# Three weight units by block at each stage boundary, and new work lists for ScalarE, VectorE and GpSimd around the first and last feed-forward tile

## The chip, the cores and the metric

The kernel runs on one core of one Trainium2 chip. TensorE multiplies, ScalarE (ACT in the profile), VectorE (DVE) and GpSimd (POOL) compute elementwise, SyncE (SP) issues the DMAs. Each engine works through its own list of instructions in the order of the program and waits on semaphores. The metric is the device time of one execution in microseconds; for the kernel before, three runs gave a median of 3314.09 us (3314.05 to 3314.48).

## The reference

One step of a two-layer encoder on 1024 new frames and 32 frames of a running stream (1056 columns together), model width 1024. What matters here is the frame around the two attentions, which is the same in both layers:

```python
y = o @ w_oa[i]                       # layer 0; w_ob in layer 1
r = r + rms_norm(y, g_mix_post[i])
# SwiGLU feed-forward, 2816 wide, between two norms, added to r
# gated input embedding: p @ w_ple, gated by sigmoid(norm(r) @ w_ple_gate),
# normed (g_ple_post) and added to r
```

Each norm divides a column of 1024 values by its root mean square. Layer 1 then takes keys, values and forget values from r (w_kb, w_vb, w_f) and attends once more.

## The kernel before

Everything is transposed: 128 rows of the width on the partitions, eight such tiles (`KD`), and the 1056 columns in three blocks b of 352 (`NB`, `TB`). Each float32 operand is split in two parts, high and low, and a product is three matmuls (`three`), so that one *group*, 1024 rows deep, is 24 matmuls of 352 columns. A weight unit is 128x1024: it is loaded to `wraw`, copied to `wh` (high) and subtracted to `wl` (low), mostly by GpSimd (L791, L796), in three slots.

A norm of a block passes all engines. ScalarE squares the eight tiles (L1429), the squares are added up on VectorE (L1885) or GpSimd (L818, the list `POOL_SUMS` says which) through a ring of two buffers, so that a square waits for the sum two before. `cols` (L979) has TensorE add over the partitions, `root` (L1437) takes the root on ScalarE, `inverse` (L1895, L1899) the reciprocal and a diagonal on VectorE, `spread` (L993) carries it to all partitions on TensorE. A "post" norm then scales the sublayer's output (`scaled`, L1909, VectorE), `residual` (L827, GpSimd) adds it to r. A "pre" norm of the new r needs no scaling ahead of the matmul: `high` (L1462, ScalarE) and `low` (L1924, VectorE) split r times the gain at once, the product is formed, and the reciprocal root, kept by `keep` (L1443) in `rsp`, multiplies the product afterwards (`gate`, `mul`: L2140, L2145).

The order of work is written out by hand for each engine. The stages of a layer after attention are:

- output projection, 24 groups. `PLACES` gives their order: six units over all three blocks, then units 6 and 7 block by block (`by_place`), so that block 0 finishes first and its norm can start.
- feed-forward, 22 tiles (`ffn_pe`, `ffn_act`, `ffn`). A tile is a gate group and an up group per block, with 24 `down` products (three matmuls each) of the tile before between them. `first_tile` goes block by block as the blocks' `low` parts come; the first group of `second_tile` writes the bank of the first gate product and waits for `silu(0,0)` (L1633), which has read it. `last_tile` goes block by block too and puts its own block 0 `down` products in (`E_AT2`).
- embedding, 24 short groups (`ple`, six matmuls each), interleaved with the first gate unit's groups; then the gate projection, 24 groups in the order of `PLACES`, with `scale` (L2260), `sigmoid` (L1765), `gated` (L2266).
- in layer 0, the key, forget and value projections (`kb`, `wf`, `vb`) then follow; layer 1 ends with the last norm, the last `residual` and six stores of the output.

Names such as "pre 0" below mean the pre norm of block 0.

## Time and profile before

| | |
|---|---|
| median of three runs | 3314.09 us |
| profiled execution | 3314.65 us, its span 3312.9 us |
| TensorE busy | 3077.6 us (93%) |
| VectorE, GpSimd, ScalarE busy | 2008.1, 1479.0, 979.6 us |
| mean granted TensorE clock | 0.962 of full |

The span goes from the first to the last instruction. Below, a stretch is named by its place in it in microseconds: layer 0's attention ends near 690, its feed-forward runs to about 1550, its gate projection to 1700, keys and values follow, and layer 1 repeats this from 2290 on. A wait in brackets, as in `[19.39 <-ACT ffn_act L1633]`, is idle time of that engine just before the row's instruction and what ended it.

### The profile page before, as it was taken

How to read it: one execution, taken by the hardware profiler on the slowest of the kernel's cores; microseconds unless marked ns; L12 is line 12 of the kernel's file. 1: busy time of each engine (PE TensorE's matmuls, PEld its weight loads, DVE VectorE, ACT ScalarE, POOL GpSimd, SP SyncE). 2: the span in 40 equal slices, each digit the busy share in tenths (PEclk: the TensorE clock that was granted, in tenths of full speed). 3: DMA queues.
4: the chain of work that ended last, by engine and by line, in shares of the span. 5: the costliest groups of instructions: out<-in, count | busy, mean ns of one | idle time of the engine just before them, and what ended most of it. 6: DMA issues, size and time to landing. Idle time of an engine off the chain costs nothing.

```text
span 3312.9 us, 59033 instructions
## 1 busy us (share of the span) xinstructions
PE 3077.6 (93%) x21250; PEld 2979.3 (90%) x21250; DVE 2008.1 (61%) x3637; ACT 979.6 (30%) x2248; POOL 1479.0 (45%) x963
## 2 busy tenths in 40 slices
PE   7898999997999999997888999999799999999787
PEld 6888999987999999997887888888799999999777
DVE  5555777456565565555573677754655655656555
ACT  3233666433000000003442167753300000000242
POOL 5223454464333343335565455545443333433454
PEclk9999999998999999998998999999899999999889
DMA  3387444211111111111102565622011111111101
GB/s 107 138 302 239 124 120 134 77 64 33 44 44 51 44 45 43 44 51 46 39 26 98 181 146 129 142 79 71 26 52 38 44 51 44 47 42 38 65 32 53
DMA packets 163119, 264.69 MB, mean 80 GB/s; under 512 B 95040, under 2 KB 108880, under 8 KB 162624
## 3 DMA queue, kind: packets, MB, share of 16 engines
q1 hardware_dynamic: 163008, 263.21, 25.8%
q8 instruction: 70, 1.15, 0.2%
q14 instruction: 41, 0.34, 0.0%
HBM read 197.74 MB, written 65.42 MB: 79 GB/s over the span
## 4 chain that ended last, share of the span: by engine, by line
PE 79%; DVE 7%; POOL 4%; issue 4%; ACT 3%; DMA 2%; SPq 1%; ACTq 0%; DVEq 0%; POOLq 0%
PE ps L1225 29%; PE ps L958 14%; PE ps L959 14%; PE ps L960 14%; PE ps L1135 4%; POOL pre_sums L818 2%; DVE sublayer_out L1909 1%; DVE pre_sums L1885 1%; PE ps L1105 1%; PE ps L993 1%; POOL residual L827 1%; DVE act_lo L1924 1%; PE ps L1106 1%; PE ps L979 1%; DMA kA_lo<-stage_lo 1%
## 5 line engine op out<-in xcount | busy, mean ns | idle before, releaser
L791 POOL TENSOR_TENSOR weight_hi<-weight_raw,ones 128x1024 fp32r<-128x1024 f32 x194 | 384.5, 1982 | 1243.8 <-PE ps L960 648.3
L2136 DVE TENSOR_TENSOR sublayer_out<-ps,sublayer_out 128x352 f32<-128x352 f32 x1008 | 527.8, 524 | 536.1 <-PE ps L960 527.8
L1225 PE MATMUL ps<-act_hi,weight_hi 128*128 128x352 f32 x2112 | 690.2, 327 | 54.6 <-ACT ffn_act L1633 38.5
L1225 PE MATMUL ps<-act_lo,weight_hi 128*128 128x352 f32 x2112 | 684.9, 324 | 0.0
L1225 PE MATMUL ps<-act_hi,weight_lo 128*128 128x352 f32 x2112 | 684.6, 324 | 0.0
L958 PE MATMUL ps<-act_hi,weight_hi 128*128 128x352 f32 (+2 forms) x1392 | 472.0, 339 | 46.2 <-POOL weight_lo L796 19.8
L796 POOL TENSOR_TENSOR weight_lo<-weight_raw,weight_hi 128x1024 fp32r<-128x1024 f32 x201 | 498.2, 2478 | 24.5 <-ACT weight_hi L1623 9.3
L858 POOL TENSOR_TENSOR probs<-probs,row_inv 128x1024 f32<-128x1024 f32 (+8 forms) x288 | 310.6, 1092 | 351.5 <-DVE row_inv L2083 351.4
L959 PE MATMUL ps<-act_lo,weight_hi 128*128 128x352 f32 (+2 forms) x1392 | 456.9, 328 | 0.0
L960 PE MATMUL ps<-act_hi,weight_lo 128*128 128x352 f32 (+2 forms) x1392 | 456.5, 328 | 0.0
L1225 PEld LDWEIGHTS ps<-act_hi,weight_hi 128*128 128x128 f32 x2112 | 400.3, 190 | 58.6 <-issue 50.5
L1225 PEld LDWEIGHTS ps<-act_lo,weight_hi 128*128 128x128 f32 x2112 | 401.2, 190 | 1.4 <-issue 1.0
L1225 PEld LDWEIGHTS ps<-act_hi,weight_lo 128*128 128x128 f32 x2112 | 400.7, 190 | 0.4 <-issue 0.2
L958 PEld LDWEIGHTS ps<-act_hi,weight_hi 128*128 128x128 f32 (+2 forms) x1392 | 265.5, 191 | 59.3 <-issue 37.4
L2088 DVE TENSOR_TENSOR probs_t_lo<-ps,probs_t_hi 128x512 fp32r<-128x512 f32 (+3 forms) x448 | 220.2, 498 | 95.6 <-ACT probs_t_hi L1587 92.7
L958 PE MATMUL ps<-probs_t_hi,v_hi 128*64 128x128 f32 (+2 forms) x1248 | 272.6, 246 | 1.4 <-DVE act_lo L2095 0.9
L959 PEld LDWEIGHTS ps<-act_lo,weight_hi 128*128 128x128 f32 (+2 forms) x1392 | 266.3, 191 | 5.9 <-issue 1.8
L960 PEld LDWEIGHTS ps<-act_hi,weight_lo 128*128 128x128 f32 (+2 forms) x1392 | 265.5, 191 | 2.9
L1633 ACT ACTIVATE ffn_act<-ps 128x352 f32<-128x352 f32 x132 | 61.4, 465 | 653.9 <-DVE ps L2140 653.9
L960 PE MATMUL ps<-probs_t_hi,v_lo 128*64 128x128 f32 (+2 forms) x1248 | 242.2, 221 | 0.0
L959 PE MATMUL ps<-probs_t_lo,v_hi 128*64 128x128 f32 (+2 forms) x1248 | 241.9, 221 | 0.0
L1578 ACT ACTIVATE probs<-ps,neg_max 128x1024 f32<-128x1024 f32 (+8 forms) x288 | 204.4, 710 | 99.5 <-DVE neg_max L2075 89.9
(168 smaller groups left out, 6201.2 us busy)
## 6 DMA issues: line engine op xcount, KB each, us to landing
weight_raw<-units SPq DMA_DIRECT2D x201, 512.0 KB, 3.3
k_hi<-kB_hi SPq DMA_DIRECT2D x32, 328.0 KB
qA_hi<-stage_hi SPq DMA_DIRECT2D x16, 528.0 KB, 2.7
qA_lo<-stage_lo SPq DMA_DIRECT2D x16, 528.0 KB, 4.0
q_hi<-qA_hi SPq DMA_DIRECT2D x16, 528.0 KB
q_lo<-qA_lo SPq DMA_DIRECT2D x16, 528.0 KB
kA_hi<-stage_hi SPq DMA_DIRECT2D x8, 656.0 KB, 3.0
kA_lo<-stage_lo SPq DMA_DIRECT2D x8, 656.0 KB, 4.6
```

Source lines behind the costliest of these rows:

```text
L791: pool.tensor_tensor(wh[:, slot, :], wraw[:, slot, :], ones[:, 0:1].to_broadcast((P, UW)), ALU.mult).then_inc(w_hi[slot], 1)
L796: pool.tensor_tensor(wl[:, slot, :], wraw[:, slot, :], wh[:, slot, :].bitcast(F32), ALU.subtract).then_inc(w_rdy[slot], 1)
L818: pool.tensor_tensor(sum_tile(key), sum_tile(key), square_tile(key, j), ALU.add).then_inc(n_add[1], 1)
L858: pool.tensor_tensor(p, p, rinv[0:M, k:k + 1].to_broadcast((M, KEYS[tile])), ALU.mult).then_inc(at_p, 1)
L958: nc.tensor.matmul(out, ah, bh, start=first, stop=False)
L959: nc.tensor.matmul(out, ah, bl, start=False, stop=False)
L960: return nc.tensor.matmul(out, al, bh, start=False, stop=last)
L1135: mm = nc.tensor.transpose(ps[0:kr, 4 + c % 2, j * P:j * P + M], pr[0:M, PROB_AT[tile] + kt * P:PROB_AT[tile] + kt * P + kr], ident[0:M, 0:M])
L1225: mm = nc.tensor.matmul(ps[:, 3 * slot + b, 0:TB], a, x, start=(k == 0 and pas == 0), stop=(k == KD - 1 and pas == 2))
L1578: nc.scalar.activation(pr[0:M, PROB_AT[tile]:PROB_AT[tile] + KEYS[tile]], score_tile(tile), ACT.Exp, bias=nmx[0:M, k:k + 1], accum_out=rsu ...
L2088: last = V.tensor_tensor(dst, src, hi.bitcast(F32), ALU.subtract)
L2136: V.tensor_tensor(y[:, m, c], src, y[:, m, c], ALU.add).then_inc(f_acc, 1)
```

## The change

The change keeps every matmul of the feed-forward and of the projections, and every load. It alters orders and who does some of the elementwise work:

- `PLACES`: five units over all blocks, then units 5, 6 and 7 by block. `cols` and `spread` of the post norms stand at other products.
- Pre norms of the stages s2, s3, s5, s6: ScalarE squares blocks 0 and 1 in turn, with block 1 in the other ring; GpSimd adds blocks 0 and 2 of s2 and s5 and block 0 of s3 and s6, VectorE the rest. In s4 block 1 goes to VectorE.
- First tile: `cols` and `spread` of pre 0 leave it and stand, with those of pre 1, ahead of the second tile. `silu(0,0)` comes before the last squares of block 2.
- Last tile: gate 0, gate 1, up 0, up 1, gate 2, up 2. `down` of block 2 alternates with `scaled` of block 0 on VectorE and with three `ple` groups on TensorE. VectorE makes the low parts of the two `pe` units, ScalarE the high part of the first `pg` unit, GpSimd its low part before the sums of post 2.
- ScalarE gets one more activation, a square root of one column, in the last tile. It also makes the high parts of more units (`split_high`), GpSimd keeps their low parts.
- In layer 0's end `vb` 0 is multiplied by its gain later, after the sums of pre 2.

```diff
-PLACES = [(m, b) for m in range(6) for b in range(NB)] + [(m, b) for b in range(NB) for m in (6, 7)]
+LATE = (5, 6, 7)
+PLACES = [(m, b) for m in range(LATE[0]) for b in range(NB)] + [(m, b) for b in range(NB) for m in LATE]
...
+    if _s in ALTERNATE:
+        SQUARES += [((_s, "pre", b), j) for j in range(KD) for b in range(2)] + [((_s, "pre", 2), j) for j in range(KD)]
...
+def ring_of(key):
+    s, kind, b = key
+    return "pre" if kind == "pre" and not (b == 1 and s in ALTERNATE) else "post"
...
+LAST_ORDER = [(0, 0), (0, 1), (1, 0), (1, 1), (0, 2), (1, 2)]
```

GpSimd ahead of the feed-forward (`tail_pool`):

```diff
-                split(0, u[0], (lin_rd, unit_done(lin, 5)))
                 residual((f"s{s}", "post", 0))
+                low(0, u[0])
+                residual((f"s{s}", "post", 1), 0, 4)
                 low(1, u[1])
-                residual((f"s{s}", "post", 1))
+                residual((f"s{s}", "post", 1), 4)
                 residual((f"s{s}", "post", 2))
                 adds((f"s{s}", "pre", 0))
-                adds((f"s{s}", "pre", 1))
+                low(0, u[0] + 1)
+                adds((f"s{s}", "pre", 2))
```

TensorE, ahead of the second tile:

```diff
+                    cols((s, "pre", 0))
+                    spread((s, "pre", 0))
+                    cols((s, "pre", 1))
+                    spread((s, "pre", 1))
```

TensorE, after the last tile's gate and up groups:

```diff
-                    for d in range(KD, 2 * KD):
+                    for d in range(KD, 3 * KD):
                         down(f, par, d, True)
-                        if d == KD + 3:
+                        if d == KD + 4:
                             cols((key, "post", 0))
...
+                        if d in (2 * KD + 2, 2 * KD + 4, 2 * KD + 6):
+                            ple(0, (d - 2 * KD - 2) // 2)
+                    spread((key, "post", 1))
```

TensorE, second gate unit:

```diff
-                place(gate, 1, 0, among=[(2, do(spread, pre[1])), (6, do(cols, pre[2]))])
-                place(gate, 1, 1, among=[(2, do(spread, pre[2]))])
-                place(gate, 1, 2)
+                place(gate, 1, 0, among=[(4, do(cols, pre[0]))])
+                place(gate, 1, 1, among=[(0, do(spread, pre[0])), (4, do(cols, pre[1]))])
+                place(gate, 1, 2, among=[(0, do(spread, pre[1])), (6, do(cols, pre[2]))])
+                spread(pre[2])
```

ScalarE, last tile:

```diff
+                for m in range(4):
+                    y_square(0, m)
+                silu(f, 2)
+                split_high(0, u[0], (fg_rd, 3 * (f0 + NF)))
+                nc.scalar.activation(epsc[:, 1:2], epsc[:, 0:1], ACT.Sqrt)
```

VectorE, after the last tile:

```diff
+                inverse(post[0])
+                for j in range(KD):
+                    down(NF - 1, 2 * KD + j, last=True)
+                    scaled(post[0], j, j + 1)
```

VectorE, last entries ahead of the feed-forward:

```diff
                 inverse(pre[0])
-                adds(pre[2])
+                for j in range(6, KD):
+                    add(pre[1], j)
+                inverse(pre[1])
```

ScalarE at the start of layer 0's feed-forward, before: from the last `act_hi` copies of r to the first silu (`ffn_act`). `pre_sums` and `pre_squares` are squares of a pre norm, `root` and `pre_rstd` are `root` and `keep`.

```order
L1462 ACTIVATE act_hi<-residual,gains 128x352 x12
L1429 ACTIVATE pre_sums_90<-residual 128x352
L1429 ACTIVATE pre_squares<-residual 128x352 x7
L1429 ACTIVATE pre_sums_90<-residual 128x352
L1429 ACTIVATE pre_squares<-residual 128x352 x3
L1437 ACTIVATE root<-ps,eps_col 88x4
L1429 ACTIVATE pre_squares<-residual 128x352 x4
L1443 ACTIVATE pre_rstd<-ps 128x352
L1429 ACTIVATE pre_sums_90<-residual 128x352
L1429 ACTIVATE pre_squares<-residual 128x352 x7
L1633 ACT_TABLE_LOAD
L1633 ACTIVATE ffn_act<-ps 128x352
```

The same place after the change, from the last weight copy on (`post_squares` is here the ring of block 1):

```order
L1452 ACTIVATE pre_sums_90<-residual 128x352
L1452 ACTIVATE pre_squares<-residual 128x352 x2
L1460 ACTIVATE root<-ps,eps_col 88x4
L1466 ACTIVATE pre_rstd<-ps 128x352
L1452 ACTIVATE pre_squares<-residual 128x352 x2
L1460 ACTIVATE root<-ps,eps_col 88x4
L1452 ACTIVATE pre_squares<-residual 128x352
L1466 ACTIVATE pre_rstd<-ps 128x352
L1656 ACT_TABLE_LOAD
L1656 ACTIVATE ffn_act<-ps 128x352
L1452 ACTIVATE pre_squares<-residual 128x352 x2
L1656 ACTIVATE ffn_act<-ps 128x352
```

Before, all squares of block 2 stand ahead of the first silu. After, six of them do, in two pieces between the roots of blocks 0 and 1, and two follow it; the pairs of blocks 0 and 1 stand above.

GpSimd between the last feed-forward tile and the gate projection of layer 0, before:

```order
L818 TENSOR_TENSOR post_sums<-post_sums,post_squares 128x352 x7
L796 TENSOR_TENSOR weight_lo<-weight_raw,weight_hi 128x1024
L818 TENSOR_TENSOR post_sums<-post_sums,post_squares 128x352 x7
L827 TENSOR_TENSOR residual<-residual,sublayer_out 128x352 x8
L796 TENSOR_TENSOR weight_lo<-weight_raw,weight_hi 128x1024
L818 TENSOR_TENSOR post_sums<-post_sums,post_squares 128x352 x7
L827 TENSOR_TENSOR residual<-residual,sublayer_out 128x352 x8
L791 TENSOR_TENSOR weight_hi<-weight_raw,ones 128x1024
L796 TENSOR_TENSOR weight_lo<-weight_raw,weight_hi 128x1024
L827 TENSOR_TENSOR residual<-residual,sublayer_out 128x352 x8
L818 TENSOR_TENSOR pre_sums_91<-pre_sums_91,pre_squares 128x352 x7
```

and after:

```order
L834 TENSOR_TENSOR post_sums<-post_sums,post_squares 128x352 x14
L843 TENSOR_TENSOR residual<-residual,sublayer_out 128x352 x8
L812 TENSOR_TENSOR weight_lo<-weight_raw,weight_hi 128x1024
L834 TENSOR_TENSOR post_sums<-post_sums,post_squares 128x352 x7
L843 TENSOR_TENSOR residual<-residual,sublayer_out 128x352 x16
L834 TENSOR_TENSOR pre_sums_91<-pre_sums_91,pre_squares 128x352 x7
L807 TENSOR_TENSOR weight_hi<-weight_raw,ones 128x1024
```

Two `weight_lo` (the `pe` units) and one `weight_hi` leave GpSimd. The low part of the first gate unit moves from behind `residual` of block 1 to behind that of block 0, and the sums of post 2 now all stand ahead of `residual` of block 1.

## Rows read from the trace of the kernel before

**Rows 1.** the page: the span

```profile
span 3312.9 us, 59033 instructions
```

**Rows 2.** TensorE's waits over the span: total, times, longest

```profile
PE ps L1225 <- ACT ffn_act L1633: 38.5, 2, 19.4
PE ps L993 <- DVE rstd_diagonal L1899: 33.5, 14, 5.8
```

**Rows 3.** stretches: length, busy per engine (instructions), clock, DMA share, GB/s

```profile
1527.00:1631.00 104.00, 76.29 (x390) 70.81 (x390) 63.14 (x101) 50.99 (x113) 70.40 (x59) 0.79 0.16 57
1684.00:1773.00 89.00, 69.42 (x385) 57.16 (x383) 60.87 (x90) 40.36 (x81) 68.17 (x56) 0.87 0.03 9
```

**Rows 4.** the same view, the steady feed-forward

```profile
790.00:1470.00 680.00, 679.79 (x4240) 679.50 (x4239) 404.29 (x713) 59.51 (x122) 256.57 (x116) 1.00 0.13 44
```

**Rows 5.** TensorE's timeline: start, us, instruction [idle before it <-releaser]

```profile
778.35 0.63 PE L1225 MATMUL ps<-act_hi,weight_hi 128*128 128x352 f32 x1 [19.39 <-ACT ffn_act L1633]
```

**Rows 6.** ScalarE's timeline, opening of layer 0's feed-forward

```profile
745.46 0.59 ACT L1462 ACTIVATE act_hi<-residual,gains 128x352 fp32r<-128x352 f32 x1 [0.59 <-POOL residual L827]
...
749.31 0.50 ACT L1429 ACTIVATE pre_squares<-residual 128x352 f32<-128x352 f32 x1 [0.69 <-POOL pre_sums L818]
...
770.00 0.50 ACT L1429 ACTIVATE pre_squares<-residual 128x352 f32<-128x352 f32 x1 [1.64 <-DVE pre_sums L1885]
...
785.09 1.28 ACT L1633 ACT_TABLE_LOAD   x1
786.38 0.46 ACT L1633 ACTIVATE ffn_act<-ps 128x352 f32<-128x352 f32 x1
```

**Rows 7.** VectorE's timeline there

```profile
736.36 2.06 DVE L1909 SCALAR_TENSOR_TENSOR sublayer_out<-sublayer_out,gains,ps 128x352 f32<-128x352 f32 x4 [1.16 <-PE ps L993]
...
763.30 6.67 DVE L1885 TENSOR_TENSOR pre_sums<-pre_sums,pre_squares 128x352 f32<-128x352 f32 x3 [0.18 <-ACT pre_squares L1429]
...
781.51 0.17 DVE L1895 RECIPROCAL rstd<-root 88x4 f32<-88x4 f32 x1 [2.69 <-ACT root L1437]
781.72 0.52 DVE L1899 TENSOR_TENSOR rstd_diagonal<-ident,rstd 88x352 f32<-88x352 f32 x1
```

**Rows 8.** GpSimd's timeline there

```profile
737.92 7.50 POOL L827 TENSOR_TENSOR residual<-residual,sublayer_out 128x352 f32<-128x352 f32 x7
746.90 7.04 POOL L818 TENSOR_TENSOR pre_sums<-pre_sums,pre_squares 128x352 f32<-128x352 f32 x6 [1.48 <-ACT pre_squares L1429]
...
764.95 2.50 POOL L796 TENSOR_TENSOR weight_lo<-weight_raw,weight_hi 128x1024 fp32r<-128x1024 f32 x1
```

**Rows 9.** TensorE's timeline, end of layer 0's feed-forward (last row: layer 1)

```profile
1530.74 0.43 PE L958 MATMUL ps<-ffn_hi_odd,weight_hi 128*128 128x352 f32 x1 [3.67 <-DVE sublayer_out L2136]
...
1577.47 0.63 PE L958 MATMUL ps<-act_hi,weight_hi 128*128 128x352 f32 x1 [7.76 <-issue]
...
1612.70 1.54 PE L993 MATMUL ps<-rstd_diagonal,ones 88*128 88x352 f32 x2 [5.45 <-DVE rstd_diagonal L1899]
...
3164.13 0.63 PE L958 MATMUL ps<-act_hi,weight_hi 128*128 128x352 f32 x1 [7.77 <-issue]
```

**Rows 10.** GpSimd's timeline there

```profile
1572.61 2.17 POOL L791 TENSOR_TENSOR weight_hi<-weight_raw,ones 128x1024 fp32r<-128x1024 f32 x1
...
1593.43 7.45 POOL L818 TENSOR_TENSOR pre_sums<-pre_sums,pre_squares 128x352 f32<-128x352 f32 x7 [7.71 <-ACT pre_squares L1429]
```

**Rows 11.** VectorE's timeline there

```profile
1603.52 8.49 DVE L1885 TENSOR_TENSOR pre_sums<-pre_sums,pre_squares 128x352 f32<-128x352 f32 x5
...
1635.30 0.53 DVE L2260 TENSOR_TENSOR ps<-ps,pre_rstd 128x352 f32<-128x352 f32 x1 [1.43 <-PE ps L960]
```

**Rows 12.** TensorE's timeline, keys of layer 0

```profile
1747.44 1.54 PE L993 MATMUL ps<-rstd_diagonal,ones 88*128 88x352 f32 x2 [5.76 <-DVE rstd_diagonal L1899]
```

**Rows 13.** GpSimd's timeline there

```profile
1770.29 2.57 POOL L796 TENSOR_TENSOR weight_lo<-weight_raw,weight_hi 128x1024 fp32r<-128x1024 f32 x1
```

**Rows 14.** TensorE's timeline, last norm of layer 1

```profile
3297.31 1.33 PE L979 MATMUL ps<-ones,post_sums 128*88 128x1 f32 x8 [5.27 <-DVE post_sums L1885]
```

## What the change is predicted to do

> **What bounds the kernel now.** I read the page first: the span is 3312.9 us [rows 1], TensorE is busy for 93% of it, and the chain that ended last is 79% TensorE. So the matmuls are the bound except where TensorE sits idle. The stretches come next. In the steady feed-forward 4240 matmuls take 679.79 of 680 us, 0.160 us each, at full clock [rows 4]: nothing is to be had there, and the change leaves it alone. Between the stages it is otherwise: TensorE is busy for 76.29 of 104 us at the end of layer 0's feed-forward (granted clock 0.79 on average) and for 69.42 of 89 us at the keys (0.87) [rows 3]. The list of waits names the largest: 38.5 us in two waits for a silu, up to 19.4 us, and 33.5 us in 14 waits for the diagonal of a norm [rows 2]. Both are in the norms between the stages, where ScalarE, VectorE and GpSimd pass small work to each other. The timelines then say why.
>
> **Opening of the feed-forward (twice).** TensorE stands for 19.39 us before the second tile at 778.35 [rows 5]; the reader sees that it waits for `silu(0,0)`, which frees the bank. ScalarE's list has all squares of block 2 ahead of it, and VectorE's sums between them go in steps of about 2.3 us (three from 763.30 in 6.67 us), in step with GpSimd's weight operations (one 2.50 us from 764.95) [rows 7, 8], so ScalarE's square at 770.00 waits 1.64 us [rows 6].
> After the change I walk the same chain. Post 2 is scaled at 736.36 before [rows 7]. Three units by block give the earlier blocks one more group (24 x 0.160 = 3.8 us) of cover, but `cols` of post 2 moves from product 12 to 28 and VectorE has sums and `low` before it; I get 734, so 2.4 earlier. The last copy of r ends at 745.46 + 0.59 - 2.4 = 743.6 [rows 6]. Then seven pairs of sums for blocks 0 and 1: GpSimd alone takes 7.04 / 6 = 1.17 us per sum [rows 8]; with VectorE's sum beside it I take 1.3 (bounds 1.17 and, if each pair went by a weight operation, 2.50). 7 x 1.3 = 9.1, two squares first 0.8, and two weight copies moved to ScalarE about 1 beyond what the ring hides: 754.5. From there `cols` (1.33 at most [rows 14], I take 0.8 at full clock), the root 0.3 (four columns, less than the silu's 0.46), reciprocal and diagonal 0.17 + 0.52 [rows 7], `spread` 0.8 (half of the two in 1.54 [rows 9]): 757.1. VectorE has two sums of block 1 left behind `inverse` of pre 0, beside one weight operation of GpSimd (up to 2.50): 759.3. `cols` of pre 1: 760.1. Its root is queued behind two squares of block 2, which wait for GpSimd's first sums after that weight operation: this is the wait that the change adds, and `keep` of pre 1 and the silu are behind it; 760.7. Diagonal, `spread`, `keep`: 762.7. Table load 1.28, silu 0.46 [rows 6]: 764.4. So the second tile starts **14 us** earlier, though the first tile, without `cols` and `spread` of pre 0 and the wait for post 2, ends only about 6 earlier than 778.35 - 19.39 = 759.0, and TensorE still waits about 11 us. Bounds: 7 x (2.50 - 1.3) = 8.4 less, so 5.6; and 16 if the sums go at 1.17 and the copies are hidden. Weights for it are ready: `low` of slot 0 comes right after the sums of pre 0. What is late next is `cols` of pre 2 at product 6, perhaps 0.5 us, and it is within the 14. Layer 1 repeats it: its wait is the other half of the 38.5 [rows 2]. Term: 28, bounds 11 and 32.
>
> On ScalarE's table loads: the row at 785.09 takes 1.28 us and the next activation starts at 786.38 [rows 6], so a switch costs 1.28 here. The Trainium skill, "ScalarE: Activation LUTs", section "What ACT_TABLE_LOAD costs", gives about 1283 ns and a drain of about 1380 ns more for each switch. By that page the silu would come 1.4 us later in each layer and the sum would be about 3 us less. The trace shows the load and no drain, so the sum goes by 1.28.
>
> **End of the feed-forward and embedding (twice).** Before, TensorE waits 3.67 us at 1530.74 (block 2's high part stands behind block 0's squares), 7.76 at 1577.47 for the first gate unit's weights, whose GpSimd work starts only at 1572.61, and 5.45 at 1612.70 for the diagonal of pre 0 [rows 9, 10]. The sums of pre 1 on VectorE, five of them over 8.49 us from 1603.52, come after those of pre 0, seven in 7.45 us from 1593.43 [rows 10, 11]. The third gate unit's first group starts one group before its `scale` at 1635.30, so at 1631.4 [rows 11]; I compare that point.
> After: the last tile's products end at about the same 1527. High part 2 still waits for block 0's squares, but these start earlier: about 1.5 of the 3.67 stay. VectorE gets two 1024-column subtractions that the trace doesn't show on VectorE; the bounds are 0.52 (a 352-column one [rows 7]) and 2.50 (GpSimd's own [rows 8]), I take 1.2 each, nearer to the first since it is the same engine. `down` of block 2 alternates with `scaled`, 8 x 1.0 us, and ends at 1546, some 3 us earlier with three `ple` groups done. The first gate unit's weights are ready at about 1550, so the 7.76 goes; what is late next is the sums of post 2, at 1559 to 1564, since the last five squares are queued behind eight `take`s of `ple` results. GpSimd then does `residual` of block 1 at about 1.07 each (7.50 / 7 [rows 8]): 1568 to 1572, then of block 2: 1576 to 1581. The copies and `take`s follow, and ScalarE squares pairs 3 to 7 only after the last `take` of block 2 (1582 at full clock). Sums of pre 0 done at 1588, and only then GpSimd's two operations for gate unit 1, ready at 1593: TensorE waits about 5 there. The rest (`cols`, `spread`, the sums of pre 1 and pre 2 beside three weight splits) gives 1610 to 1612 for the third unit's start at full clock. At half clock all through, 144 `ple` and 144 gate matmuls would cost 0.16 more each, 46 us, of which I find half hidden in the waits above: 1634. Some waits end on a slow matmul (0.63 for the first after the 7.76), others on a fast one (0.43) [rows 9], and the mean clock was 0.79 [rows 3]; I take a third of the way: 1618, **13 us** earlier. Bounds: -3 and 21. Layer 1 is the same stage with the same waits (7.77 at 3164.13 [rows 9]). Term: 26, bounds -5 and 42.
>
> **Keys in layer 0.** TensorE waits 5.76 us for the diagonal of pre 0 at 1747.44 [rows 12]. After, `cols` of post 1 moves to an earlier place of its unit and waits longer by about 2 (one more `scaled` half and a table load lie before its sum), the second key unit's weights come late (about 3), and `residual` of block 2 stands behind five sums. Pre 1 goes to VectorE, so the last `spread` comes about 9 earlier. But `vb` 0's gain now stands behind the sums of pre 2: gain, split, gain, split (six operations of 128x1024 at 2.17 to 2.57 each, 13 in all [rows 8, 10, 13]) end at about 1768, where they ended at 1772.9 [rows 13]. Both are needed for the value groups. Term: 5, bounds -4 (the weights' 2.57 twice and a waiting sum more) and 9.
>
> **Last norm.** The third unit's cover lets the sum before `cols` at 3297.31, with a wait of 5.27 [rows 14], come about 1 us earlier; after it nothing changes. Term: 1, bounds 0 and 2.
>
> **Sum.** 28 + 26 + 5 + 1 = 60. The profiled execution took 3314.65 us, 0.56 above the median of 3314.09; 3314.65 - 60 = 3254.65, and as a median 3254. All terms at a bound would be 2 and 85, which don't fall together.
>
> **Rivals.**
> *The end of the feed-forward gives nothing.* For it: GpSimd is left with one list, in which sums of post 2, three residuals, sums of pre 0 and the gate unit's weights now stand in one line, and a `take` there waits for a residual that waits for the sums. Against: the 7.76 and 5.45 waits have their causes removed. It gives 3254 + 24 = 3278.
> *The clock stays full and the sums overlap freely.* Twice 16 and twice 19, keys 8, last norm 1: 79 less, 3235. Against it: TensorE still waits some 11 us at each opening.
> *The port.* Slower than before: VectorE's and GpSimd's sums, now side by side, hold each other up. For it: VectorE's 2.3 us steps above. Against: these were beside 2.50 us operations; GpSimd's residuals slowed only to 1.07. There are five places with seven pairs. If a pair cost 1.3 + x in place of 1.3, 35x reaches 60 at x = 1.7, so it decides from 3.0 us a pair on. With a GpSimd weight operation and a sum one after the other, 2.50 + 7.45 / 7 = 3.56 [rows 8, 10], it gives 35 x 2.26 = 79 against 60: 3333.
> The Trainium skill, "SBUF — State Buffer", section "Who interferes with whom", states the mechanism: a VectorE instruction with two SBUF inputs and a GpSimd instruction that reads SBUF exclude each other for the whole instruction. By that rule the trace agrees as to the steps, and a pair would cost the two durations one after the other, 1.06 + 0.52 = 1.6, not 3.56; with 1.6 the sum would be 10 less.
> *The change doesn't do what it says*, since another wait of the same size (weights for the second tile, or block 2's sums) takes the silu's place: only the other terms are left, 32, so 3282.
>
> **Chances.** Forecast (a gain of 45 to 75) 0.58; the end gives nothing 0.14; free overlap 0.15; another wait at the opening 0.08; the port 0.02; smaller gains or none of several causes 0.03. What a measurement can tell from no change is 0.2%, 6.6 us. Slower by more than that 0.03, within it 0.03, faster 0.94. The range takes in the first two rivals: 3230 to 3284.
>
> **What would show it.** TensorE's wait before the second tile should be about 11 us, not 19.4, in both layers, and end on a silu about 14 us earlier after the attention's end. VectorE's sums of pre 1 at the opening should come at about 1.3 us each beside GpSimd's. The 7.76 wait should be gone, and a wait of some us for GpSimd's weights should be at gate unit 1. `cols` of post 1 in layer 0's gate projection should wait longer than before. If the pairs take over 2 us, or the wait before the second tile stays above 17, the walk of the first term is wrong; if the third gate unit starts less than 5 us earlier after the last tile, the second is.

## The result and the profile after

The changed kernel takes 3262.60 us (median of 4 runs, 3261.40 to 3267.74) against 3314.28 us (4 runs, 3314.05 to 3315.22) of the kernel before in the same series: 51.7 us less, a ratio of 0.9844 with a 95% interval of 0.9832 to 0.9856. The forecast was 3254 with a range of 3230 to 3284. The time is in the range, 8.6 us above the forecast, but the sum came out near it partly by luck. The stages that the forecast counted on gave 34.6 us in place of its 60: the opening was put too high, and keys and last norm went the other way. What brought the total near was a gain of 16 us in a stage to which the forecast had given nothing.

The page of the kernel after begins with its span; 46.9 us less than in [rows 1].

```profile
span 3266.0 us, 59087 instructions
```

TensorE's waits over the span, in total, how many, longest. They answer to [rows 2].

```profile
PE ps L975 <- POOL weight_lo L812: 24.8, 8, 15.0
PE ps L996 <- DVE post_sums L1951: 23.7, 7, 6.0
PE ps L1010 <- DVE rstd_diagonal L1965: 22.6, 11, 7.0
PE ps L975 <- issue: 14.7, 3, 7.1
...
PE ps L1261 <- ACT ffn_act L1656: 4.8, 2, 2.4
```

The 38.5 us for a silu are down to 4.8, and the 33.5 us for a norm's diagonal to 22.6. The stretches of [rows 3], from the last products of the last tile to the third gate unit (now 90 us long, 104 before), and the 89 us ahead of the value products:

```profile
1514.00:1604.00 90.00, 70.24 (x390) 65.10 (x390) 62.82 (x96) 47.03 (x104) 67.86 (x57) 0.89 0.18 66
1665.00:1754.00 89.00, 64.68 (x354) 54.17 (x352) 63.20 (x90) 36.33 (x77) 62.10 (x47) 0.85 0.08 29
```

The first holds the same 390 matmuls in 14 us less, at a granted clock of 0.89 and not 0.79. In the second TensorE is busy for less of the time than before: the keys have become worse.

Where the time went is best read from milestones, each the same instruction in both traces. Four of the anchors in after, and one in before, from TensorE's timeline: the start of attention (302.03 and 305.76), the second tile, the third gate unit and the value products.

```profile
302.03 0.80 PE L958 MATMUL ps<-k_hi,q_hi 128*128 128x512 f32 x1 [9.68 <-DVE q_turned L2046]
```

```profile
305.76 0.80 PE L975 MATMUL ps<-k_hi,q_hi 128*128 128x512 f32 x1 [9.67 <-DVE q_turned L2112]
...
773.15 0.63 PE L1261 MATMUL ps<-act_hi,weight_hi 128*128 128x352 f32 x1 [2.42 <-ACT ffn_act L1656]
...
1604.24 0.63 PE L975 MATMUL ps<-act_hi,weight_hi 128*128 128x352 f32 x1 [2.96 <-DVE sublayer_out L2356]
...
1754.18 0.55 PE L975 MATMUL ps<-weight_hi,act_hi 128*128 128x256 f32 x1 [0.60 <-issue]
```

The profiled execution of after is 3.7 us late at the attention already, ahead of all that the change touches (it is also the slowest of its four). So stages are compared by their length, and whole traces from this start to the end of the span: 3010.9 us before, 2960.2 after, 50.7 less.

| stage (layer 0 / layer 1) | before, us | after, us | difference | predicted |
|---|---|---|---|---|
| opening: output projection to second tile | 153.8 / 153.5 | 144.7 / 144.9 | -17.7 | -28 |
| second tile to the last tile's own first `down` (1515.56 before, 1502.40 after) | 737.2 / 737.8 | 729.3 / 729.5 | -16.3 | 0 |
| from there to the `scale` of the third gate unit's first group (1635.30, 1609.79) | 119.7 / 119.9 | 107.4 / 107.7 | -24.5 | -26 |
| from there to the value products (layer 0) | 139.0 | 144.4 | +5.4 | -5 |
| from there to the last norm's scaling (layer 1) | 79.0 | 81.2 | +2.2 | -1 |

The sum is -50.9; layer 1's attention took 0.2 more.

### The profile page after: what moved, and what is told of

It reads as the page before. It is cut to its first block, busy times and chain, and to the rows that moved or that the text cites. A ratio compares the mean times of both kernels' runs of the same rounds, so it can differ in the third digit from the quotient of the medians.

```text
span 3266.0 us, 59087 instructions
## 1 busy us (share of the span) xinstructions
PE 3078.8 (94%) x21250; PEld 2982.2 (91%) x21250; DVE 1998.0 (61%) x3648; ACT 979.1 (30%) x2255; POOL 1450.5 (44%) x943
## 4 chain that ended last, share of the span: by engine, by line
PE 82%; DVE 7%; issue 3%; ACT 2%; POOL 2%; DMA 2%; SPq 1%; ACTq 0%; DVEq 0%; POOLq 0%
PE ps L1261 30%; PE ps L975 15%; PE ps L976 14%; PE ps L977 14%; PE ps L1152 4%; DVE sublayer_out L1975 1%; PE ps L1122 1%; PE ps L996 1%; PE ps L1010 1%; PE ps L1123 1%; DVE act_lo L1990 1%; POOL pre_sums L834 1%; DMA kA_lo<-stage_lo 1%; DVE pre_sums L1951 1%; DVE stage_lo L2071 1%
## 5 line engine op out<-in xcount | busy, mean ns | idle before, releaser
L807 POOL TENSOR_TENSOR weight_hi<-weight_raw,ones 128x1024 fp32r<-128x1024 f32 x185 | 366.5, 1981 | 1187.8 <-PE ps L977 616.3
L812 POOL TENSOR_TENSOR weight_lo<-weight_raw,weight_hi 128x1024 fp32r<-128x1024 f32 x197 | 486.9, 2471 | 38.9 <-ACT weight_hi L1646 24.4
```

Of the source, the lines that this page charges most:

```text
L807: pool.tensor_tensor(wh[:, slot, :], wraw[:, slot, :], ones[:, 0:1].to_broadcast((P, UW)), ALU.mult).then_inc(w_hi[slot], 1)
L812: pool.tensor_tensor(wl[:, slot, :], wraw[:, slot, :], wh[:, slot, :].bitcast(F32), ALU.subtract).then_inc(w_rdy[slot], 1)
```

## The experiments

All were timed beside the kernel before. "From the attention's start" is the span minus the start of the row that [..q_turned] releases, as above; two executions of the same kernel differ by up to 7 us in it, so single traces are read by stage, where they agree better.

**e1: only the place of a wait, in the kernel before.** The trace of before has a gap that no term of the prediction spoke of. TensorE's timeline there, and GpSimd's:

```profile
1483.24 0.63 PE L1225 MATMUL ps<-act_hi,weight_hi 128*128 128x352 f32 x1 [5.24 <-issue]
```

```profile
1480.64 2.50 POOL L796 TENSOR_TENSOR weight_lo<-weight_raw,weight_hi 128x1024 fp32r<-128x1024 f32 x1
```

```
-                    for slot in range(2):
-                        pe.wait_ge(w_rdy[slot], f + (u[slot] + 1))
                     for b in range(NB):
                         for slot in range(2):
+                            pe.wait_ge(w_rdy[slot], f + (u[slot] + 1))
                             products(f, slot, b, 24 * (2 * b + slot), among)
```

> The kernel before, with one thing changed: in the last feed-forward tile TensorE waits for the up projection's weights (slot 1) right ahead of its first up group, and no longer ahead of all groups. Theory A (TensorE's 5.24 us of 'issue' at 1483.24 are that wait: GpSimd's weight_lo of slot 1 ends at 1480.64 + 2.50 = 1483.14): one gate group of 24 matmuls, 3.86 us, runs in it, so 1.4 us of the wait stay, and most of the 1.9 us of half clock behind it go; 4 to 6 us in each layer, 8 to 12 in all: 3302 to 3306 us, and in the trace no wait over 2 us there. Theory B (the 5.24 us are a stall of instruction supply or of the clock, not a wait for weights): within 2 us of before, and the gap stays.

Measured: 3303.18 us (3298.36 to 3305.66), ratio 0.9964 [0.9950, 0.9978]. From the second tile to the last tile's `down` wait 730.7 and 730.6 us, where before has 737.2 and 737.8: 13.8 less in both layers. Two stretches of e1 over the place of the gap (columns as in [rows 3]):

```profile
1476.00:1480.00 4.00, 4.00 (x27) 4.00 (x26) 3.40 (x4) 0.50 (x1) 3.92 (x3) 1.00 0.31 73
1480.00:1484.00 4.00, 3.94 (x25) 3.65 (x24) 2.56 (x7) 0.00 (x0) 2.33 (x1) 1.00 0.70 231
```

and of before over it:

```profile
1478.00:1482.00 4.00, 0.00 (x1) 0.00 (x0) 2.35 (x4) 0.50 (x1) 3.92 (x3) 0.80 0.56 197
1482.00:1486.00 4.00, 2.76 (x9) 2.79 (x10) 0.00 (x0) 0.00 (x0) 1.14 (x1) 0.50 0.58 197
```

The gap is gone, and with it the half clock behind it (0.50 in before, 1.00 in e1). Theory A holds. Nothing is left of the wait, not 1.4 us: the first group carries `down` products of the tile before among its own, so it covers more than its 24 x 0.160 us. "Issue" in the list of waits was a wait for weights; it ends 0.10 us after GpSimd's `weight_lo` (1480.64 + 2.50). Of the 13.8 us by stage, 10.8 arrive in the time: in the trace of e1 the next stage is 1.9 and 0.7 us longer than in before (121.6 and 120.6), the keys' 4.2 (143.2), and only part of that is made up by shorter openings (151.1 and 152.0).

**e2: the same wait, put back in the kernel after.**

```
+                    for slot in range(2):
+                        pe.wait_ge(w_rdy[slot], f + (u[slot] + 1))
                     for n, (slot, b) in enumerate(LAST_ORDER):
-                        pe.wait_ge(w_rdy[slot], f + (u[slot] + 1))
                         products(f, slot, b, 24 * n, among)
```

> The kernel after, with the wait for both slots' weights back ahead of all groups of the last feed-forward tile; the new order of the groups stays. Theory A (the order of the waits gives the last tile's 8 us in each layer): about 7 us a layer come back, so 14 over after: 3276 to 3279 us, and the gap of about 5.2 us is there again, named 'issue' or weight_lo. Theory B (the new order of groups, or another edit, gives it): within 3 us of after, 3260 to 3266.

Measured: 3273.87 us (3267.98 to 3275.60), ratio 0.9878 [0.9862, 0.9894]; 11 over after. From the attention's start 2970.8. The stage is 736.3 and 735.4 us long again, and its trace has the gap:

```profile
1471.63 0.63 PE L1261 MATMUL ps<-act_hi,weight_hi 128*128 128x352 f32 x1 [5.24 <-issue]
```

Theory A, from the other side: 12.9 us by stage, and by time 11 and not the 14 that it gave. To the order of the groups by itself and to the other edits is left what separates this stage of e2 from before's, 0.9 and 2.4 us. The order lets two gate groups run ahead of the first up group; e1 shows that one is enough for the wait for the up weights.

**e3: two units by block at the gate projections and before's lists for the keys and the last norm.**

```
 LATE = (5, 6, 7)
+GATE_LATE = (6, 7)
...
+            unit("kb", 0, ("pg0", 5))
...
-            unit_low("kb", 0)
...
+            adds(("s4", "pre", 1))
             adds(("s4", "pre", 2))
```

> The kernel after, with two units by block (6, 7) at the gate projections and the lists of before for layer 0's keys and the last norm; the output projections keep three units. Theory A (by the two traces this part of the change costs 5.4 us at the keys and 2.2 at the last norm): 7 us less than after, about 3255 us. Theory B (these losses come from what is left over of the earlier stages, for instance from the shifted start of the gate projection, and not from this part): within 2 us of after, 3261 to 3265. What was predicted for this part alone was a gain of 6, so 3269 without it.

Measured: 3260.16 us (3254.89 to 3266.33), ratio 0.9843 [0.9829, 0.9857], from the attention's start 2953.8, 6.4 less than after and 1.3 less than its second execution (e12). By time the two can't be told apart (3262.60 in another series); by stage the keys' part is 141.8 us, and 142.3 in e8, which has the same lists. Nine traces with the lists of after (both of after, e2, e4 to e7, e9, e11) lie between 144.1 and 144.5. With before's lists there are four values: 139.0, 143.2 (e1), 141.8 and 142.3. So this part of the change costs 1 to 5 us at the keys, about 2.8 in the mean. The last norm's stage is 79.0, 79.0, 80.5 and 80.3 us with before's lists; with after's it is 81.1 to 81.3 in six traces and 79.6 or 79.7 in three, about 1 us more in the mean. The sign of theory A is borne out at the keys, its size half; at the last norm the two ranges overlap.

**e4: two units by block at the output projections only.**

```
-LATE = (5, 6, 7)
+LATE = (6, 7)
+GATE_LATE = (5, 6, 7)
...
-                take(5, 1)
+                take(6, 1)
...
-                high(pre[0], 0, 2)
...
+                high(pre[0], 0, 3)
```

> The kernel after, with two units by block (6, 7) at the output projections only, with the lists of before up to the scaling of the last post norm; pairs of sums and everything behind stay. Theory A (three units by block moved the scaling of post 2 not at all, 736.67 against 736.36 by the trace, and cost 1.4 us at the start of the first tile): within 2 us of after, or up to 3 less: 3260 to 3264 us. Theory B (as predicted, three units give the scaling 2.4 us of lead in each layer): 4 to 6 us more than after, about 3267.

Measured: 3270.94 us (3266.82 to 3272.01), ratio 0.9868 [0.9852, 0.9884]; from the attention's start 2966.1, 5.9 more than after. The openings take 148.0 and 149.4 us. Theory A falls: after's are 144.7 and 144.9, and the sixteen openings of after's code in eight traces have a mean of 143.9, so three units are worth about 5 us in each layer, at least 3 in any pair of executions. Theory B gave 4 to 6 in all and not by layer, and for a lead of the scaling that isn't there.

The scaling of post 2 comes 113.0 us after the output projection's start in e4, 112.1 in after (110.9 in e12) and 111.8 in before (109.1 in e1). So it has not moved forward, and that is why two traces alone made the third unit look worthless. What it waits for is TensorE's `spread`. In after, and below it in e4, ScalarE's root of post 2 and TensorE's `spread` behind it:

```profile
737.27 0.26 ACT L1460 ACTIVATE root<-ps,eps_col 88x4 f32<-88x4 f32 x1 [5.18 <-PE ps L996]
...
739.75 0.76 PE L1010 MATMUL ps<-rstd_diagonal,ones 88*128 88x352 f32 x2
```

```profile
734.45 0.26 ACT L1468 ACTIVATE root<-ps,eps_col 88x4 f32<-88x4 f32 x1 [8.29 <-PE ps L1004]
...
738.53 0.76 PE L1018 MATMUL ps<-rstd_diagonal,ones 88*128 88x352 f32 x2
```

The root waits for TensorE's `cols`, not for a weight copy on ScalarE, and `spread` starts without a wait: the change has it at product 44 of the first tile (before: 24), and the diagonal lay ready for 1.5 us in after, for 3.1 in e4. In e4 TensorE gets there later since it waits for `act_lo` on the way (1.10, 0.43, 0.44 us), with matmuls 0.29 us apart behind that; and VectorE has twelve `low` left behind the scaling, 10.98 us, where after has ten in 8.65.

**e5: the end of the feed-forward and the embedding as before.** (Diff: the blocks of TensorE's, ScalarE's, VectorE's and GpSimd's programs between the last tile's products and the second gate unit are those of before; its core is)

```
-ALTERNATE = ("s2", "s3", "s5", "s6")
+ALTERNATE = ("s2", "s5")
...
-                unit_low(gate, 0)
+                slot, use, _ = USES[gate, 0]
+                split(slot, use, (fd_rd, 24 * (f0 + NF)))
...
+                    row_squares(pre[1], m, m + 1)
-                pair_squares(3, KD)
```

> The kernel after, with the stage between the last tile and the second gate unit as before: the order of down, cols and spread after the last tile, the places of the embedding groups, ScalarE's, VectorE's and GpSimd's lists there, and the sums of this stage's pre norm not in pairs. The last tile's new order of groups and waits stays. Theory A (this part is worth the 12.3 us in each layer that the two traces show from the last tile to the third gate unit): about 24 us over after, measured from the start of the attention, where the traces of after stands at 2960.2 us before the end: 2984; as a time about 3287. Theory B (part of these 12 us is owed to the last tile's new order, which comes first in the same stretch): 12 to 18 us over after.

Measured: 3285.44 us (3281.62 to 3287.98), ratio 0.9915 [0.9900, 0.9930], 23 over after; from the attention's start 2977.0, 17 over. The two measures disagree, and the stage decides: it takes 119.2 and 119.4 us, against 107.4 and 107.7, so 23.5 us in both layers. Of the 6.7 us between the two, 4.2 are this execution's short openings, in code that is not changed (142.0 and 143.4). Theory A holds; the wait for the first gate unit is back:

```profile
1559.43 0.63 PE L978 MATMUL ps<-act_hi,weight_hi 128*128 128x352 f32 x1 [8.04 <-issue]
```

**e6 and e11: the second gate unit's weights on ScalarE and VectorE.** In after TensorE stands for 7.04 us at 1582.67, called issue; GpSimd's timeline says for what:

```profile
1582.67 0.63 PE L975 MATMUL ps<-act_hi,weight_hi 128*128 128x352 f32 x1 [7.04 <-issue]
```

```profile
1576.21 2.09 POOL L834 TENSOR_TENSOR pre_sums<-pre_sums,pre_squares 128x352 f32<-128x352 f32 x2
1578.26 1.89 POOL L807 TENSOR_TENSOR weight_hi<-weight_raw,ones 128x1024 fp32r<-128x1024 f32 x1
1580.23 2.34 POOL L812 TENSOR_TENSOR weight_lo<-weight_raw,weight_hi 128x1024 fp32r<-128x1024 f32 x1
```

```
-                for j in (1, 2):
-                    slot, use, _ = USES[gate, j]
-                    split(slot, use, (pe_rd, 24 * layer + (20, 24)[j - 1]))
+                slot, use, _ = USES[gate, 2]
+                split(slot, use, (pe_rd, 24 * layer + 24))
...
-                pair_squares(3, KD)
+                pair_squares(3, 5)
+                slot, use, _ = USES[f"pg{layer}", 1]
+                split_high(slot, use, (pe_rd, 24 * layer + 20))
+                pair_squares(5, KD)
...
+                ple_low(1, "pg")
                 add(pre[1], 5)
```

> The kernel after, with the split of the second gate unit's weights taken from GpSimd (where it stands behind the sums of pre 0 and ends at 1582.57) and given to ScalarE (high part, between two pairs of squares) and VectorE (low part, before its sixth sum of pre 1). Theory A (TensorE's 7.04 us of 'issue' at 1582.67 are the wait for that split): the wait falls to under 1 us, GpSimd's next split ends earlier and no longer lies beside VectorE's diagonal and sums, and the third gate unit starts 5 to 7 us earlier in each layer: 10 to 14 us less than after, 2946 to 2950 from the start of the attention. Theory B (the norm's chain of pre 0 to pre 2 sets the third unit's start, the weights don't): the 7.04 goes and comes back as a longer wait at 1604.24; within 3 us of after.

> The kernel of e6 once more, beside the kernel after in one and the same series, for an interval between the two: 15 to 19 us less than after.

Measured: e6 3244.82 us (3242.33 to 3254.40), ratio 0.9799 [0.9783, 0.9814]; e11 3250.95 (3247.15 to 3252.92), 0.9805 [0.9792, 0.9819], and after in e11's series 3260.83, 0.9842 [0.9829, 0.9856]. The intervals don't meet: it is better than after by 10 us in the one series that holds both (e11), which is less than the 15 to 19 expected; e6 lies 18 under after's time of another series. From the attention's start 2943.4 and 2950.2. Five rows of e6:

```profile
1567.49 1.05 ACT L1645 ACTIVATE weight_hi<-weight_raw 128x1024 fp32r<-128x1024 f32 x1
```

```profile
1568.95 1.22 DVE L2226 TENSOR_TENSOR weight_lo<-weight_raw,weight_hi 128x1024 fp32r<-128x1024 f32 x1
...
1575.37 4.84 DVE L1953 TENSOR_TENSOR pre_sums<-pre_sums,post_squares 128x352 f32<-128x352 f32 x2
```

```profile
1575.15 2.55 POOL L812 TENSOR_TENSOR weight_lo<-weight_raw,weight_hi 128x1024 fp32r<-128x1024 f32 x1
```

```profile
1570.27 0.40 PE L974 MATMUL ps<-act_hi,weight_hi 128*128 128x352 f32 x1 [0.89 <-issue]
```

The wait is 0.89 us, 6.2 less; the stage is 6.6 us (e6) and 4.3 us (e11) shorter than in after in layer 0, 7.8 and 1.9 in layer 1. VectorE's last two sums of pre 1 now take 4.84 us beside GpSimd's weight operations for the third unit, where after has them in 3.33 (the seven sums from 1582.75, without such a neighbour, 4.29 us for all). Theory A as to the wait, and in e6 as to the size. Why e11, the same kernel, keeps so much less is not shown.

**e7: the low part of the second tile's gate weights on VectorE.**

```
-                low(0, u[0] + 1)
...
+                V.tensor_tensor(wl[:, 0, :], wraw[:, 0, :], wh[:, 0, :].bitcast(F32), ALU.subtract).then_inc(w_rdy[0], 1)
                 ffn(layer)
```

> The kernel after, with the low part of the second tile's gate weights (GpSimd, 2.4 us, between its sums of pre 0 and pre 2) given to VectorE behind the diagonal of pre 1. Theory A (this GpSimd operation holds up VectorE's diagonal, 1.30 us in place of 0.52, and its last two sums of pre 1, 2.41 in place of 1.1, which are on the path to the second tile): the second tile starts about 2 us earlier in each layer, 4 us less than after in all, 2956 from the start of the attention. Theory B (no hold-up: both have these lengths for another reason, as GpSimd's sums that follow): no gain, or 1 us more by VectorE's own 1.2 us in each layer.

Measured: 3258.66 us (3254.18 to 3265.14), ratio 0.9835 [0.9820, 0.9850]; openings 144.5 and 143.1 us, after's 144.7 and 144.9, in its second execution (e12) 143.2 and 141.8. No gain. The hold-up itself was real, as VectorE's timelines in after and in e7 show:

```profile
762.90 1.30 DVE L1965 TENSOR_TENSOR rstd_diagonal<-ident,rstd 88x352 f32<-88x352 f32 x1
764.12 2.41 DVE L1951 TENSOR_TENSOR pre_sums<-pre_sums,post_squares 128x352 f32<-128x352 f32 x2
```

```profile
757.80 1.22 DVE L1964 TENSOR_TENSOR rstd_diagonal<-ident,rstd 88x352 f32<-88x352 f32 x1
758.95 1.14 DVE L1950 TENSOR_TENSOR pre_sums<-pre_sums,post_squares 128x352 f32<-128x352 f32 x2
762.90 0.17 DVE L1960 RECIPROCAL rstd<-root 88x4 f32<-88x4 f32 x1 [2.81 <-ACT root L1459]
```

The two sums go from 2.41 to 1.14 us, and the reciprocal behind them then waits 2.81 us for ScalarE's root and not 1.72: `cols` of pre 1 now waits for ScalarE's copy of pre 0's factor out of the same PSUM bank (0.65 us <- pre_rstd in TensorE's timeline). That the bank is what it waits for is read from the kernel, not tested. From `cols` of pre 0 to `cols` of pre 1 it takes 4.78 us in e7 and 5.01 in after: the path had a second limit 0.2 us below the first. The diagonal of pre 0 itself stays at 1.22 us, now beside two of GpSimd's sums. Theory B has the right size without its reason: the hold-up of the two sums was real, the cover was not seen.

**e8: e3, e6 and e7 together.** (Diff: those of the three.)

> After with three edits together: two units by block at the gate projections with the keys' and last norm's lists of before (6.4 us less by its trace), the second gate unit's weights split on ScalarE and VectorE, and the second tile's low part on VectorE. Theory A (the three are independent and each is worth what its own theory says): 6.4 + 12 + 4 = 22 us less than after, 2938 from the start of the attention, about 3240 as a time. Theory B (only the first holds): 6 less, about 3256.

Measured: 3246.98 us (3241.78 to 3249.18), ratio 0.9793 [0.9780, 0.9807]; from the attention's start 2945.9. That is e6 within what can be told; the 6 us of e3 and the 4 that e7 was given are not in it. Neither theory: the keys' stage has e3's length (142.3). What separates e6's 2943.4 from e11's 2950.2, one kernel, is as large as what e3 gives, so whether the two add up stays open.

**e9: the sums of pre 0 and pre 1 in turn again.**

```
-ALTERNATE = ("s2", "s3", "s5", "s6")
+ALTERNATE = ("s3", "s6")
...
                 adds((f"s{s}", "pre", 0))
+                adds((f"s{s}", "pre", 1))
                 low(0, u[0] + 1)
-                adds((f"s{s}", "pre", 2))
```

> The kernel after, with the sums of pre 0 and pre 1 at the openings of the feed-forward in turn on GpSimd, as before, and those of pre 2 on VectorE; everything else of the opening stays (no cols and spread in the first tile, weight copies on ScalarE, three units by block). Theory A (pairs on two engines are what shortens the wait before the second tile, 1.4 us for a pair against 1.17 for each sum in turn): GpSimd has 14 sums one after the other, 16.4 us against the 10 measured in after, and ScalarE's and GpSimd's other work adds little: the second tile 6 to 8 us later in each layer, 12 to 16 over after, 2972 to 2976 us from the start of the attention. Theory B (the gain of the opening comes from the other edits, the pairs give nothing since GpSimd and VectorE hold each other up): within 3 us of after.

Measured: 3280.51 us (3278.99 to 3282.74), ratio 0.9900 [0.9885, 0.9915], 18 to 20 over after; from the attention's start 2977.2. The openings take 155.7 and 153.3 us, as long as before (153.8 and 153.5; in e1 151.1 and 152.0). TensorE's timeline, ahead of the second tile at 778.48:

```profile
765.95 1.54 PE L1010 MATMUL ps<-rstd_diagonal,ones 88*128 88x352 f32 x2 [9.50 <-DVE rstd_diagonal L1965]
...
774.52 1.54 PE L1010 MATMUL ps<-rstd_diagonal,ones 88*128 88x352 f32 x2 [5.08 <-DVE rstd_diagonal L1965]
```

Theory A, with 2 to 3 us a layer more than I gave it, since ScalarE's root of pre 0 also stands behind all squares of pre 1. Without the pairs, and the order of squares that goes with them, nothing of the opening's gain is left. That e4 also takes 4.8 us a layer of it away means that the edits don't add up one by one; the new places of `cols` and `spread` were not tried alone.

**e10: e6, with three squares of pre 2 ahead of the root of pre 1 at the keys.**

```
+            row_squares(pre[2], 0, 3)
             root(pre[1])
-            row_squares(pre[2], 0, 3)
```

> The kernel of e6 with one swap more: at layer 0's keys ScalarE does its first three squares of pre 2 before the root of pre 1, not behind it. Theory A (GpSimd stands idle for 9.10 us in after since these squares are queued behind that root, and TensorE then waits 4.3 us for the sums of pre 2): GpSimd's sums start about 5 us earlier and the 4.3 us wait goes: 4 us less than e6, about 3240 us. Theory B (the root, or the diagonal of pre 1, comes so much later by the three squares and by GpSimd's sums beside VectorE's, that it takes the place of the wait): within 2 us of e6.

Measured: 3249.03 us (3246.78 to 3253.19), ratio 0.9804 [0.9790, 0.9817]; e11 in the same series 3250.95. Nothing that can be told is gained, as theory B had it, but for another reason than it gave. GpSimd's timeline:

```profile
1719.23 2.01 POOL L834 TENSOR_TENSOR pre_sums<-pre_sums,pre_squares 128x352 f32<-128x352 f32 x2 [5.86 <-ACT pre_squares L1451]
1724.80 5.22 POOL L834 TENSOR_TENSOR pre_sums<-pre_sums,pre_squares 128x352 f32<-128x352 f32 x5 [3.56 <-ACT pre_squares L1451]
```

The idle 9.10 us are split into 5.86 and 3.56: the first two sums come earlier, the other five still wait for squares that stand behind the copy of pre 1's factor. The sum's end, and TensorE's wait of 4.32 us for it, stay.

**e12: the kernel after once more.**

> The kernel after once more, unchanged. In its first profile the attention started 3.7 us later than in before (305.76 against 302.03 us) although nothing ahead of it is changed. Theory A (this start differs from one execution to the next): another value here, and 2958 to 2962 us from it to the end, as in the first. Theory B (the change causes it): 305 to 306 again.

Measured: 3260.83 us (3257.02 to 3265.22), from the attention's start at 300.08 us to the end 2955.1. The start is the execution's own (299.3 to 305.8 over fourteen traces of kernels that are alike up to there): theory A; but the 2955.1 lie below the 2958 to 2962 that it gave. The openings took 143.2 and 141.8 us, so this stage too differs by 2 to 3 us between executions of one kernel, and most of that lies in its first 70 us, ahead of TensorE's part in any norm: the first `cols` comes 73.5 us after the start in after's layer 0, where 19 matmuls of that stretch are 0.29 us apart, and 70.7 in e12's, where one is; the stage from the second tile (729.5 and 728.9), that of the end (107.7 and 106.7) and the keys (144.3) repeat within 1.

## Why the prediction came out right, and which steps of it were wrong

**Opening: predicted 28, measured 17.7.** Over all traces with the opening of before (e1 too: mean 152.6) and of after (mean 143.9) it is 17.5 in both layers, with single pairs of executions between 14 and 22. The mechanism is the one named: TensorE's single wait of 19.4 us falls apart into five. TensorE's timeline in after:

```profile
761.58 0.79 PE L996 MATMUL ps<-ones,pre_sums 128*88 128x1 f32 x8 [1.26 <-POOL pre_sums L834]
764.25 1.54 PE L1010 MATMUL ps<-rstd_diagonal,ones 88*128 88x352 f32 x2 [1.89 <-DVE rstd_diagonal L1965]
766.59 1.34 PE L996 MATMUL ps<-ones,pre_sums 128*88 128x1 f32 x8 [0.80 <-DVE pre_sums L1951]
769.19 1.54 PE L1010 MATMUL ps<-rstd_diagonal,ones 88*128 88x352 f32 x2 [1.26 <-DVE rstd_diagonal L1965]
```

and at 773.15 the 2.42 above: 7.6 us of waits, where I expected about 11. The failed step is the first of the walk, the scaling of post 2: "I get 734, so 2.4 earlier". VectorE's timeline in after, which answers to the first row of [rows 7]; 3.9 is to be taken off, since the output projection starts at 628.45 and not at 624.57:

```profile
740.55 4.02 DVE L1975 SCALAR_TENSOR_TENSOR sublayer_out<-sublayer_out,gains,ps 128x352 f32<-128x352 f32 x8 [1.26 <-PE ps L1010]
```

So 736.7, not 734 (735.4 in the second execution). The third unit does pay (e4), but not here: I had priced the new place of `cols` and VectorE's list ahead of it, and not that `spread` now stands at product 44 of the first tile. TensorE enters that tile 103.2 us after the projection's start (101.9 in before) and reaches `spread` at 111.3, when the diagonal has been ready for 1.5 us. The pairs came out nearly as predicted. GpSimd's timeline has, and VectorE's beside it:

```profile
751.45 3.69 POOL L834 TENSOR_TENSOR pre_sums<-pre_sums,pre_squares 128x352 f32<-128x352 f32 x3 [1.86 <-ACT pre_squares L1452]
755.33 0.99 POOL L834 TENSOR_TENSOR pre_sums<-pre_sums,pre_squares 128x352 f32<-128x352 f32 x1 [0.19 <-ACT pre_squares L1452]
758.09 2.14 POOL L834 TENSOR_TENSOR pre_sums<-pre_sums,pre_squares 128x352 f32<-128x352 f32 x2 [1.77 <-ACT pre_squares L1452]
760.59 0.93 POOL L834 TENSOR_TENSOR pre_sums<-pre_sums,pre_squares 128x352 f32<-128x352 f32 x1 [0.35 <-ACT pre_squares L1452]
```

```profile
753.06 4.28 DVE L1951 TENSOR_TENSOR pre_sums<-pre_sums,post_squares 128x352 f32<-128x352 f32 x4
```

GpSimd has seven sums in 7.75 us, 1.11 each (I took 1.3, by [rows 8]), and 2.3 us of waiting for ScalarE between them (I took 1). VectorE's go at 1.07 beside them, and at 0.57 without a neighbour (e7): VectorE is the one slowed, and GpSimd sets the pace. From `cols` of pre 0 to the second tile it took 11.6 us and not 9.9 (11.4 to 11.6 in all traces with the pairs, 22.5 to 23.3 in the others); e7 shows that two limits lie there side by side. The port as a rival is refuted for sums beside sums: it needed 3.0 us a pair.

The Trainium skill, "SBUF — State Buffer", section "Who interferes with whom", has such instructions of VectorE and GpSimd exclude each other for their whole length. Beside a GpSimd weight operation the trace agrees (2.41 us for two sums, 1.14 without it in e7); beside GpSimd's sums a pair cost 1.11 us, no more than GpSimd's 1.17 alone, and not the 1.6 that I had worked out from the rule. That VectorE's sums are held up, 1.07 in place of 0.57 us, agrees with it; that the two durations add up does not.

ScalarE's table load is as predicted, 1.28 us, and the silu starts 0.01 us behind it:

```profile
771.25 1.28 ACT L1656 ACT_TABLE_LOAD   x1
772.54 0.46 ACT L1656 ACTIVATE ffn_act<-ps 128x352 f32<-128x352 f32 x1
```

**Last tile: predicted 0, measured 16.3.** The step that failed is the sentence "After: the last tile's products end at about the same 1527". I had read the steady feed-forward only up to 1470 [rows 4], where TensorE never waits, and took the rest for alike; the gap at 1483.24 stood behind this window, and the list of waits called it issue. e1 and e2 show that 13 to 14 us of the 16.3 are this one wait and the half clock behind it, in both layers. That this gain stood in for what the opening and the keys lacked is luck.

**End of the feed-forward and embedding: predicted 26, measured 24.5** (e5: 23.5). Right, mechanism and size: the 7.76 of [rows 9] is gone, the wait for GpSimd's weights at the second unit is there, 7.0 and not 5 us, and the granted clock rose from 0.79 to 0.89. How much the clock and how much the waits give of the 24.5 was not separated. (By its own terms the lower bound should have been -6, twice -3, and not -5.) The point of [rows 11] lies now at

```profile
1609.79 0.53 DVE L2350 TENSOR_TENSOR ps<-ps,pre_rstd 128x352 f32<-128x352 f32 x1 [1.81 <-PE ps L977]
```

**Keys: predicted 5 less, measured 5.4 more** (1 to 5 more by the spread of before, e1, e3 and e8). The waits that I named came, `cols` of post 1 waits 5.54 us in place of 2.74, but the gain against them did not. What failed is "Pre 1 goes to VectorE, so the last `spread` comes about 9 earlier". TensorE's timeline in after, answering to [rows 12], and VectorE's:

```profile
1726.69 1.54 PE L1010 MATMUL ps<-rstd_diagonal,ones 88*128 88x352 f32 x2 [6.96 <-DVE rstd_diagonal L1965]
...
1740.48 1.34 PE L996 MATMUL ps<-ones,pre_sums 128*88 128x1 f32 x8 [4.34 <-POOL pre_sums L834]
```

```profile
1717.43 8.57 DVE L1951 TENSOR_TENSOR pre_sums<-pre_sums,pre_squares 128x352 f32<-128x352 f32 x6 [0.18 <-ACT pre_squares L1452]
```

The last `spread` came 135.4 us after this stage's start, where it had come after 131.7 (135.8 in e1, which has before's lists): not earlier at all. VectorE's sums of pre 1 take 1.43 us each, the first of them beside GpSimd's weight operations, the diagonal of pre 0 stands behind them in VectorE's list, and GpSimd, relieved of these sums, has nothing to do for 9.10 us until ScalarE's squares of pre 2 come.

**Last norm: predicted 1 less, measured 2.2 more.** The wait for the last sum is 6.0 us, not 5.27 [rows 14]. That the third unit moved `cols` nearer to the norm's work before it is a reading of the order, not tested. By the spread under e3 the change here is between 1 us less and 2 more, about 1 more in the mean.

The rival "the end of the feed-forward gives nothing" falls with e5, "another wait of the same size" with the 7.6 us above, and "the clock stays full" with the granted clock of 0.89 at the end of the feed-forward and with the time, 28 us over its 3235.

## What to carry to other kernels

A gap called "issue" in a chain of well-named waits can be a wait like the others; here it was one for weights (e1, e2, e6). So look what ended on the other engines just before the row starts, and read every stage to its last instruction, also the one that is steady in the middle. A wait for two buffers at the head of a block costs whatever the later one costs; asked for at its first use, it is covered by the work on the first, and that edit of two lines, made alone in the kernel before, gave 10.8 us by time, a fifth of the whole change's gain. Taking work off an engine pays only up to the next limit on the path (e7, e10), and it is that second limit, not the length of what was moved, that should be priced.

## What the runs showed of the hardware

A wait of 5.24 us on TensorE cost about 7 (6.5 and 7.2 by stage in e1): the matmuls behind it came 0.29 us apart and not 0.16 for some 4 us, with a granted clock of 0.50 in that stretch against 1.00 in e1. VectorE subtracts a 128x1024 weight tile in 1.22 us where GpSimd takes 2.3 to 2.7 in the stages shown; I had taken 1.2 from bounds of 0.52 and 2.50.
